# First block's attention re-planned: values in the array's column halves, one probability copy a unit, convolution in pieces

## What is computed

```python
z = hp @ w_in
c_q, c_kv, k_pe, gate_b, gate_c, x_in = jnp.split(z, SPLITS, axis=-1)
...
attn = causal_block_attention(q_nope, q_rope, k_nope, k_rope, v)     # 8 heads, 96 wide, values 64 wide
u = gate_c * x_in
y = sum(conv_w[k] * u_pad[:, k:k + plen] for k in range(CONV_W))
conv = gate_b * y                                                     # 512 channels
merged = jnp.concatenate([rms_norm(attn[:, PAD_FRONT:], attn_out_norm),
                          rms_norm(conv[:, PAD_FRONT:], conv_out_norm)], axis=-1)
return merged @ w_out
```

## Time and profile before

| | |
|---|---|
| median of 3 runs | 681.85 us (681.42 to 682.8) |
| the profiled execution | 682.93 us, its span 681.1 us |
| mean granted TensorE clock | 0.977 |
| busy share of the span | TensorE 93%, VectorE 52%, ScalarE 43%, GpSimd 7% |
| chain that ended last | TensorE 70%, DMA 15%, VectorE 8%, ScalarE 5% |

### The profile page before, as it was taken

One profiled execution on the slowest core, in us unless ns is written; L12 is line 12 of the kernel. 1 busy time (PEld: TensorE's weight loads), 2 busy tenths in 40 slices (PEclk: granted clock), 3 DMA queues, 4 the chain that ended last, 5 costly groups with the idle time before them and its releaser, 6 DMA issues.

```text
span 681.1 us, 10146 instructions
## 1 busy us (share of the span) xinstructions
PE 633.6 (93%) x3995; PEld 477.4 (70%) x3995; DVE 357.0 (52%) x689; ACT 293.8 (43%) x560; POOL 50.7 (7%) x75
## 2 busy tenths in 40 slices
PE   8999899999999775779899999999999999999996
PEld 6979888842543321333389999898788888888885
DVE  4687663841130120110088886757856666666665
ACT  5855562421110110100085765564665555555554
POOL 3100101200010000000048100000000000000001
PEclk9999999999999978879999999999999999999998
DMA  8946337989999999999997443355535555555101
GB/s 347 418 192 256 112 159 307 417 342 424 428 396 422 421 420 421 422 421 420 423 421 306 151 152 124 124 187 186 185 131 190 191 202 193 199 193 186 63 1 62
DMA packets 26286, 180.73 MB, mean 265 GB/s; under 512 B 3184, under 2 KB 3312, under 8 KB 5120
## 3 DMA queue, kind: packets, MB, share of 16 engines
q1 hardware_dynamic: 25200, 177.60, 65.9%
q10 hardware_dynamic: 1040, 2.50, 0.9%
HBM read 179.04 MB, written 1.05 MB: 264 GB/s over the span
## 4 chain that ended last, share of the span: by engine, by line
PE 70%; DMA 15%; DVE 8%; ACT 5%; issue 2%; POOLq 0%; SPq 0%; POOL 0%; ACTq 0%; DVEq 0%
PE ps L1610 67%; DMA ring<-stream_dram 15%; PE ps L1613 3%; DVE ring_r L408 2%; ACT single L401 1%; DVE work L1545 1%; ACT work L885 1%; DVE work L1548 1%; DVE h L1598 0%; DVE single L1437 0%; ACT work L794 0%; ACT single L807 0%; DVE work L1601 0%; ACT turned L890 0%; ACT work_r L881 0%
## 5 line engine op out<-in xcount | busy, mean ns | idle before, releaser
L1610 PE MATMUL ps<-turned,single 128*128 128x256 f32 (+2 forms) x944 | 231.2, 327 | 1.6 <-ACT work L664 0.8
L1610 PE MATMUL ps<-turned,ring_r 128*128 128x256 f32 (+1 forms) x648 | 180.0, 282 | 0.0
L1610 PEld LDWEIGHTS ps<-turned,single 128*128 128x128 f32 x944 | 156.3, 189 | 18.3 <-issue 2.0
L408 DVE TENSOR_TENSOR ring_r<-ring,single 128x1024 fp32r<-128x1024 f32 (+1 forms) x132 | 160.3, 1237 | 13.5 <-ACT single L401 13.4
L401 ACT ACTIVATE single<-ring 128x1024 fp32r<-128x1024 f32 (+1 forms) x132 | 134.1, 1047 | 0.1
L1610 PEld LDWEIGHTS ps<-turned,ring_r 128*128 128x128 f32 x648 | 121.4, 189 | 0.4
L1610 PE MATMUL ps<-ring,work 128*32 128x512 f32 (+2 forms) x462 | 70.6, 618 | 17.0 <-DMA ring<-stream_dram 14.8
L1610 PEld LDWEIGHTS ps<-single 128*128 128x128 f32 x257 | 38.9, 191 | 34.5 <-issue 21.1
L1610 PE MATMUL ps<-single,turned 128*128 128x512 f32 (+3 forms) x208 | 59.4, 366 | 2.2 <-DVE turned L1225 1.5
L1610 PE MATMUL ps<-single 128*128 128x512 f32 (+1 forms) x257 | 55.8, 356 | 3.4 <-DVE single L1437 2.3
L1610 PE MATMUL ps<-single,work_r 128*128 128x512 f32 x176 | 56.3, 392 | 0.0
(11 more groups left out here) (260 smaller groups left out, 738.2 us busy)
## 6 DMA issues: line engine op xcount, KB each, us to landing
ring<-stream_dram SPq DMA_DIRECT2D x145, 1024.0 KB, 11.9
work<-stream_dram SPq DMA_DIRECT2D x12, 1024.0 KB, 12.4
turned_w<-stream_dram SPq DMA_DIRECT2D x4, 1024.0 KB, 14.9
extra<-stream_dram SPq DMA_DIRECT2D x2, 1024.0 KB, 9.6
ring<-stream_dram SPq DMA_DIRECT2D x2, 832.0 KB, 7.3
h<-x_dram SPq DMA_DIRECT2D x2, 512.0 KB, 4.4
gain<-gains_dram ACTq DMA_DIRECT2D x2, 512.0 KB, 8.6
yields<-stream_dram SPq DMA_DIRECT2D x1, 1024.0 KB, 13.7
```

The source lines that it names most:

```text
L408: dve.tensor_tensor(ring_r[:, place, a], ring[:, place, a], w_hi[k % HIGHS][:, a].bitcast(F32), ALU.subtract).then_inc(s["wlo_done"], 1)
L1610: return pe.matmul(o, lhsT, rhs, start=start, stop=stop, **kw)
```

## The change

It edits the plan of the 16 units. Values are computed once per head pair (`values(hp)`, in units 4, 8, 12 and behind the last), with a 64-wide stationary operand for each head that writes rows 0 to 63 or 64 to 127 of the bank; the key tiles are now meta, first and second (`v1[:, 0]` is the meta tile, zero below row 16), so a unit's probabilities are copied by one ScalarE instruction of 256 or 384 columns. The probabilities of the four units of a pair are kept in `pt_even` and `pt_odd`. The six convolution parts are cut into 48 triples and dealt to units 0 to 7 (`CONV_PIECES`), the 16 shares to units 9 to 15 and the end (`SHARES`); high and low copies of the convolution follow each channel group as it is done, those of groups 0 to 2 in a region of `cst` that is free at that time. GpSimd's zeroing of the padding of `pm1` and `pt1` goes away, and so do the waits on it.

```diff
-FILL = 7
+CONV_PIECES = (6, 6, 6, 7, 3, 6, 7, 7)
+SHARES = {9: ((0, 0), (0, 1), (1, 0)), 10: ((1, 1), (0, 2), (1, 2)), 11: ((0, 3), (1, 3)),
+          13: ((2, 0), (2, 1), (2, 2)), 14: ((2, 3), (3, 0), (3, 1)), 15: ((3, 2),)}
+SHARES_OUT = {12: (0, 1), 15: (2,), 16: (3,)}
...
         def share_bank(j):
-            return (5, 2)[j % 2]
+            return (5, 2, 2, 5)[j]
...
                     if n == aside[1]:
-                        sp.wait_ge(s["o_ps"], 2 * HEADS)
+                        sp.wait_ge(s["o_ps"], HEADS // 2)
...
                     act.wait_ge(s["pt_ps"], w + 1)
-                    full_k = P if w % 2 == 0 else 2 * P
-                    act.activation(pt1[:, w % 2, 0:full_k], ps[:, 3 + w % 2, 0:full_k], ACT.Copy)
-                    act.activation(pt1[0:META, w % 2, full_k:full_k + P], ps[0:META, 3 + w % 2, full_k:full_k + P],
-                                   ACT.Copy).then_inc(s["pt_sb"], 1)
+                    i, to = w % 2, (pt_even, pt_odd)[(w // 2) % 2]
+                    act.activation(to[:, 0:2 + i, i * P:(i + 1) * P],
+                                   ps[:, 3 + w % 2, 0:(2 + i) * P].rearrange("p (a b) -> p a b", b=P), ACT.Copy
+                                   ).then_inc(s["pt_sb"], 1)
...
-            def values(u):
-                hd, i = u // 2, u % 2
-                pe.wait_ge(s["pt_sb"], u + 1)
...
-                for k in range(2 + i):
-
-                    last = mm(o, v1[k][:, c:c + 2 * VD], pt1[:, i, k * P:(k + 1) * P], u % 4 == k == 0,
-                              u % 4 == 3 and k == 1 + i, skip_group_check=True)
+            def values(hp):
+
+                pe.wait_ge(s["pt_sb"], 4 * hp + 4)
+                if hp >= 2:
+                    pe.wait_ge(s["att_low"], hp - 1)
+                for k in range(NT + 1):
+                    for j in range(2):
+                        c = (2 * hp + j) * VD
+                        lo = (k // 2) * P
+                        last = mm(ps[j * VD:(j + 1) * VD, 6 + hp % 2, lo:TOK], v1[:, k, c:c + VD],
+                                  (pt_even, pt_odd)[j][:, k, lo:TOK], k == 0, k == NT, skip_group_check=True)
+                        if hp == HEADS // 2 - 1 and k == j == 0:
+                            last.then_inc(split_used, 1)
                 last.then_inc(s["o_ps"], 1)
...
-                    conv_part(6 + u)
-                if 0 <= f < 4 * NT:
-                    conv_share(f // 2, 2 * (f % 2))
-                    conv_share(f // 2, 2 * (f % 2) + 1)
...
+                if u < CONV_STEPS:
+                    for n in range(sum(CONV_PIECES[0:u]), sum(CONV_PIECES[0:u + 1])):
+                        c, t = n // DT, n % DT
...
+                        conv_piece(6 + c, t)
+                for j, m in SHARES.get(u, ()):
+                    conv_share(j, m)
...
                         if i == 0:
-                            last.then_inc(split_used, 2)
+                            last.then_inc(split_used, 1)
+                if u and u % 4 == 0:
+                    values(u // 4 - 1)
                 turn_probs(u)
-                if u:
-                    values(u - 1)
...
-            values(2 * HEADS - 1)
-            pe.wait_ge(s["cm_sb"], 2 * NT)
+            conv_share(3, 3)
+            values(HEADS // 2 - 1)
+            pe.wait_ge(s["cm_sb"], 3)
             mix_share(0, range(2 * NT))
```

More of the change, by code:

```diff
@@ L205, in two_blocks @@
         xn = cut(NT, D)
-        v1_last = cut(3 * VD * HEADS // 2)
+        pt_even = cut(NT + 1, TOK)
         top[0] = (NT + 1) * D
@@ L1170, in conv_gated, with conv_low @@
                                   ).then_inc(s["conv_done"], 1)
+            def conv_low(m):
+                dve.wait_ge(s["mrg_high"], m + 1)
+                high, low = merged(CT + m)
+                dve.scalar_tensor_tensor(low, mrg[:, m, :], vec[:, V_GCONV + m:V_GCONV + m + 1], high.bitcast(F32),
+                                         ALU.mult, ALU.subtract).then_inc(s["convg_done"], 1)
             conv_taps(0)
@@ L1683, in _, with conv_piece, conv_part @@
                         last.then_inc(s["z_ps"], 1)
-            def conv_part(c):
+            def conv_piece(c, t):
                 m, kind = c // 3, c % 3
                 lo, w = (META, TOK) if kind == 2 else (META - 2, TOK + 2)
-                chunk(ps[:, conv_bank(m, kind), 0:w], 2 + c // 2, c % 2, [x[:, :, lo:lo + w] for x in (x_hi, x_lo)],
-                      frees=1 - c % 2).then_inc(s["conv_ps"], 1)
+                at = (c % 2) * D + t * P
+                begin, last = triple(ps[:, conv_bank(m, kind), 0:w], [a[:, at:at + P] for a in split_pair(2 + c // 2)],
+                                     [x[:, t, lo:lo + w] for x in (x_hi, x_lo)], t == 0, t == DT - 1)
+                if t == 0 and c % 2 == 0:
+                    begin.then_inc(split_used, 1)
+                if t == DT - 1:
+                    last.then_inc(s["conv_ps"], 1)
+            def conv_part(c):
+                split_ready(2 + c // 2, c % 2)
+                for t in range(DT):
+                    conv_piece(c, t)
             conv_part(0)
@@ L1805, in conv_share @@
                 pe.wait_ge(s["convg_done"], m + 1)
-                if m == 0 and j >= 2:
-                    pe.wait_ge(s["cm_sb"], j - 1)
+                if m == 0:
+                    pe.wait_ge(*((s["cu_done"], CT), (s["conv_done"], CT), (s["cm_sb"], 2), (s["cm_sb"], 2))[j])
                 c = (m % 2) * D + n * 512
-                begin, last = triple(ps[:, share_bank(j), :], [x[:, CT + m, i * P:(i + 1) * P] for x in (mrg_hi, mrg_lo)],
+                begin, last = triple(ps[:, share_bank(j), :], [x[:, i * P:(i + 1) * P] for x in merged(CT + m)],
                                      [w[:, c:c + 512] for w in split_pair(8 + m // 2)], m == 0, m == CT - 1)
```

166 lines of the change are left out of this document (84 added, 82 removed).

## The result

The changed kernel takes 675.04 us (median of 4 runs, 674.77 to 675.26) beside 681.7 us for the kernel before (4 runs, 681.42 to 682.8): a ratio of 0.9896, 95% interval 0.9883 to 0.9909. On the 681.85 us of the forecast that is 674.8 us, 7.1 us less, with an interval of 6.2 to 8.0. A second measurement of the same kernel (`e8_after_again`) gave 0.9905 (0.9888 to 0.9922), 6.5 us less. The forecast was 676.3 us, 5.5 less, in a range of 675.0 to 678.4.

What follows compares the result with a forecast made beforehand. TensorE was taken to bound the 51.7 us stage of 16 units, with 2.6 us idle. Values -3.8, waits removed -2.6, waits added +1.1, fewer groups -0.2 make -5.5: 681.85 to 676.3 us, range 675.0 to 678.4.

Steps and rivals of the forecast that it cites:

- the waits removed: In the units: waits for low copies (1.5 us), gate copies (0.8) and unit 6's probabilities (0.3) go, together -2.6 us.
- Values removed and added: In the units: 40 value products (9.2 us) replaced by four pair groups of 1.34 us (5.4), so -3.8 us.
- Rival 1: In the value groups: the array halves don't overlap, values cost 9.2 us again, gain 1.7 us, 680.1 us; chance 6%.
- Rival 2: In the value groups: the array halves overlap fully, 1.15 us a pair, gain 6.3 us, 675.5 us; chance 8%.
- the 0.3 for unit 6: At unit 6's start: 0.3 us of waiting for probabilities, expected to go because the unit now has seven triples.
- Waits added: Grouped values wait for the probability copy: 0.5 us each in units 8 and 12, 0.1 at the end, +1.1 us.
- -0.2 for fewer groups: In the units: twelve fewer groups of value products, each with a wait of its own, -0.2 us.
- The cover: In the units: redealt triples and shares give VectorE and ScalarE time for softmax and side work, at no cost.
- rivals 3: In some units, above all 3, 8 and 9: softmax chain becomes the bound, takes 1.5 to 4 us; chance 8%.
- rival 5: In every unit: VectorE and ScalarE take turns; at 90% in series the time is 4 us longer, 686; chance 3%.
- Rival 4: In the weight stream: an unmoved gate holds the loads, so 681.9 us or half of the gain; chance 5%.
- the times that were named: Signs in the profile after: units end near 101.7 us, DMA restarts near 98 to 99, batch at about 131.

Runs made afterwards that it cites:

- e8_after_again: Changed kernel, unchanged, measured again on a second chip (also called e8): 675.91 us, ratio 0.9905.
- e1: Kernel before with only the change's values part (grouped values, one copy of probabilities a unit); convolution parts, shares and copies left in place: 683.88 us, ratio 1.0029.
- e10: Kernel before with high and low copies of groups 0 to 2 made early, as in e3, but group 2's low copy one iteration later: 680.95 us, ratio 0.9989.
- e4: Kernel before, unchanged, measured and profiled once more (`e4_before_again`): 681.35 us, ratio 0.9995.
- e3: Kernel before with only the convolution's high and low copies of groups 0 to 2 moved forward into their new region: 682.1 us, ratio 1.0003.
- e7: Changed kernel with two triples moved from unit 7 to 8 and one share from unit 11 to 12, ahead of the waiting values: 674.71 us, ratio 0.9882.
- e9: e1 with seven additional unused 512-column products in unit 7, ahead of the first share: 681.42 us, ratio 0.9999.
- e2: Kernel before with convolution pieces and shares dealt out as in the change, with early high and low copies, but the old per-unit values: 679.01 us, ratio 0.9959.
- e5: Changed kernel with each pair's value products in two blocks, first head then second, instead of in turn: 678.07 us, ratio 0.9938.

## Where the prediction held, and the step that failed

The mechanism came as forecast: shorter value groups, the old waits gone, two small new ones, and a weight stream that starts earlier with the end of the units. What was wrong is the size of one term, the waits removed. It was put at 2.6 us and measured about 3.7. That is 1.1 us more, of which the values, 0.3 us below their forecast, take some back; the stage gained 6.3 us for a forecast of 5.5.

**Values removed and added.** Forecast 9.2 - 5.4 = 3.8 us. Measured, five products are 1.05 us in e1's steady units, 8.4 for eight heads, and the four groups are 4 x 1.23 = 4.9: 3.5 us. Both terms were a little high and cancel nearly (0.2 of the first is rounding: 0.45 us for two products is 0.225 each, 9.0 for forty). The overlap is a factor of 2.3 / 1.23 = 1.9 with the forecast's 0.23 us a product, and 1.7, as in the earlier trace rows, with e1's 0.21. Rival 1 is out. Rival 2 was nearer on the group, 1.15 us beside the measured 1.23; that its total of 6.3 us is just what the stage gained is luck, for it had the waits at 2.6 us too.

**Waits removed: the step that failed.** "Together **-2.6 us**" took the idle times as the list gives them. In unit lengths they are 1.8 us for the low copies (e10 against e4), and for the gate copies 4.33 - 3.89 = 0.44 and 5.09 - 4.23 = 0.86, the units with such a wait against their likes without, where the list has 0.19 and 0.59. The last one, listed at 0.17, was left out of the sum as part of the next item; by the rows of e4, 105.41 less 104.62 and 0.46 for two value products, it was 0.3. With the 0.3 for unit 6, which I keep from the forecast, that is 1.8 + 1.3 + 0.3 + 0.3 = **3.7 us instead of 2.6**. Three of the listed waits stood for about 0.25 us more than their number, and the last one for 0.16. That the low copies' wait has this size is shown by e10 and e3; for the gate copies it is read off units alike in one trace, not tried.

**Waits added.** Forecast 0.5, 0.5 and 0.1. Listed are 0.33 and 0.33; from the score product's start at 78.80 with its 0.26 to 79.55 are 0.49 us, and at the end 98.38 less 97.51 and 0.70 are 0.17. So 1.15 against 1.1. By unit lengths it is a little less: e7's unit 7 to 8 lasts 2.62 us with two triples of 0.36, so 1.90 without them, against 2.31 in e8. That is 0.41 us a wait, and covering both gives 0.8 us of stage in e7. The other 0.08 belongs to the group of values then.

**The sum.** -3.5 - 3.7 + 1.15 = -6.05, and the stage is 6.3 us shorter. The forecast's -0.2 for fewer groups would make it -6.25, but no run shows that term: the 1.05 us from e1 compares units with a whole group against units without, and may hold it already. Without it some 0.25 us of the stage stay open. The cover held: no wait for a normalisation is listed in any unit, so rivals 3 and 5 did not come, but e1 shows how near they were: with half of the change the old order of side work holds TensorE for 5.4 us. Rival 4 did not come either, since the gates moved with TensorE: the batch at 129.15 stands 7.6 us earlier, 6.4 without the 1.2 us of the late start, and the 48 issues that began at 208.18 in the first profile of before begin at 200.58, 7.6 us earlier too.

**Added up part by part.** Apart from the size of the waits, the forecast's terms hold for the whole change and not for its parts. The -3.8 for the values holds only where the waits are gone too; the parts' measured -0.3 (e9) and -2.9 (e2) make 3.2, and the other 3.1 us exist only with both. In e2, 3.7 us of waits removed less one new wait of 0.81 (1.06 by the same 0.25) would be 2.6; it shows 2.9. What removes that last wait once the values are moved too was not tried; ScalarE's one copy a unit instead of two is the candidate.

**The signs and the smaller sums.** The end of the units (99.61 us), the restart of DMA (97.10) and the batch (129.15) came 1 to 2 us ahead of the times that were named, of which 1.2 is the late start of the profile that they were counted from. The new waits are listed at 0.33 us, just under the 0.4 to 0.6 that were named. In rival 5, 90% of 62.9 us is 56.6, which is 4.9 us above 51.7 and not 4. And rivals 1, 4 and 5 leave 5% for the same time and 3% for slower, where 4 and 4 are given.

## What to carry to other kernels

Price a wait by the unit with it against the same unit without it, start to start, and not by the idle time in the list: here the difference was 0.08 to 0.27 us a wait, and over the waits of before about 0.9 us of a 6 us gain. Before shortening TensorE's part of a stage with hardly any slack, ask what its side work must do in the same time: 3.5 us of products taken out gave nothing until VectorE's and ScalarE's work was dealt out anew. And let products for two halves of the array alternate in the program's order: here that was worth 0.48 us a group.

## What the runs showed of the hardware that was not expected

- Two column halves of 64 overlap nearly whole when products alternate between them: 1.23 us for 640 columns in each, where five products of 0.23 us, an estimate of full overlap from the earlier trace rows, are 1.15. The same products in two blocks take 1.71 us (e5).
- Behind a wait of 2.15 us, with TensorE busy for 0.90 and 0.62 us of the two stretches of 2 us before the fall (80 to 84 us), the granted clock was 0.50 (1.2 GHz) for about 3 us (e1), and the stage was 1.7 us longer than in e9; there, with seven products more in that wait (busy 1.70 and 1.55) it stayed at 1.00 (2.4 GHz). A wait of 1.57 us at the same place did not bring it down (`e4_before_again`).
- The start of the first block's units differs by 1.2 us between two executions of the kernel before (55.46 and 54.29 us). A comparison of two single profiles, 681.1 and 673.2 us of span, shows 7.9 us where the stage has 6.3.
